# Expert slots spread over partitions, output weights stored by column halves, and TensorE kept active before the experts

## The chip, the cores and the metric

One Trainium2 chip, of which the kernel uses one core: TensorE (PE; its weight loads are PEld), VectorE (DVE), ScalarE (ACT), GpSimd (POOL), SyncE (SP, which here only issues DMAs) and 16 DMA engines. The metric is the device time of one execution in microseconds (us). What a measurement of this kernel can tell from no change is about 0.2%, some 3 us.

## The reference

One decoder layer over 1024 tokens (and 16 meta tokens), model width 1024: attention and a gated recurrence, merged by gates; an output projection; then a hierarchical mixture of experts, and a last norm. All is float32. What matters here is the end:

```
merged = gate_m * (o_mla @ w_br_mla[l]) + gate_h * (o_hg @ w_br_hgrn[l])
h = h + merged @ w_out[l]
u = rmsnorm(h, ffn_norm[l])
h = h + hier_moe(u, ...)      # top group of 8, then the top 2 of its 8 experts
...
# hier_moe: a token's two experts e (of 64), each with w1, w3: 1024x256 and w2: 256x1024
hdn = jax.nn.silu(xb @ w1[e]) * (xb @ w3[e])
y   = (hdn @ w2[e]) * gate    # scattered back and added to the token
```

Each expert has 3 MiB of weights (2 MiB of w1 and w3, "up", 1 MiB of w2, "down"), 192 MiB in all, and they are read once from HBM. The inputs are drawn from a fixed seed, so the routing is fixed: 2048 (token, expert) pairs, on average 32 to an expert, 18 to 46.

## The kernel before

**Up to the experts.** The first half of the time goes to projections, attention and recurrence. `merge_part` makes the merged branches. `output_part` then runs over 8 tiles of 128 tokens. For a tile t, TensorE multiplies with the output weights in four quarters (`quarter`; each product is three matmuls, L130 to L132, of high and low parts; the weights' parts lie in `g.woh` and `g.wol`); quarters 0 and 1 give columns 0 to 511, quarters 2 and 3 columns 512 to 1023, and each half raises `w_mm` by one, so `w_mm` is 2t+2 when tile t is done. DVE adds the result to the residual (`add`), ACT and DVE norm it, TensorE transposes it (`turn`), multiplies with the router's weights (`logits`, L1850), and DVE and ACT choose experts and gates (`choose`, `shares`, `shared`, `valued`). The product of tile t+1 hides the routing of tile t; for tile 7 nothing hides it.

**Lists.** For each chosen pair the rank of the token within its expert is counted (`ranks`, L1858, L1859; DVE reads it in `place`). `place` compares a table of numbers with the rank and so makes a matrix with a one where the slot is; `lists` (L1865, L1867) multiplies it with the token numbers and gates. The result is a list for every expert: its slot numbers stand along the partitions, 64 to an expert (`CAP`), an even expert on partitions 0 to 63 and an odd one on 64 to 127. The table is `io128`, which holds 0 to 63 twice, so the token of rank r stands on partition r (or 64 + r).

**Experts.** `experts_part` takes two experts (a pair) at a time. GpSimd gathers the rows of a pair from `u_moe` in HBM by an indirect DMA (L1612, L2046: 128 indices, one 4 KiB row to each partition; indices beyond the range move nothing), TensorE transposes them (L2192), multiplies with w1 and w3 (L2219, 32 rows of the trace to an expert) and w2 (L2203), and GpSimd scatters the pair's results to `y_moe` by an indirect DMA (L2057). The weights come through 7 buffers (`NBUF`): `g.load_up` (two DMAs of 1 MiB, L1352) and `g.load_down` (one, L1356), both issued by SP. The first 7 experts' loads are issued in `output_part`'s `sync`; expert e+7 is loaded when expert e's products are done (`up_mm`, `dn_mm`). Each load spreads over all 128 partitions and all 16 DMA engines. After the last expert the rows of `y_moe` and `h_mid` are read back, added, normed and stored.

**Memory that holds back loads.** Up buffers 4 to 6 and down buffers 4 and 5 lie where `g.woh` and `g.wol` are, down buffers 3 and 6 where the merged tiles' parts `f_mh` and `f_ml` are. In the kernel before, none of these is loaded until `w_mm` is 16:

```
sp.wait_ge(w_mm, 2 * TT)
g.load_down(sp, 3, 3)
store_u(TT - 1)
g.load_up(sp, 4, 4)
```

**GpSimd before the first gather** writes the slot records of each tile (`record`, L1600, two indirect DMAs), clears one row buffer after tile 7's norm (L1606), waits for the lists (`rows_ok`) and gathers; a third buffer is cleared at L2028.

Of the kernel before, what the change touches and what calls it, by code (L numbers as in the profile page):

```python
# [15 lines left out]
F32 = mybir.dt.float32  # L16
# [1345 lines left out]
def merge_part(nc, g, sem):  # L1362
# [14 lines left out]
    wo_src = g.w_out[0].rearrange("(j p) n -> p j n", p=P)  # L1377

# [42 lines left out]
    def scalar(act):  # L1421
        def high(n):
            if n >= 2:
                act.wait_ge(mm_ok, done(n - 2, 1))
                act.wait_ge(w_in[n % 2], 16 * ((n - 2) // 2) + 16)
            act.activation(wh[n % 2][:, :, :], w[n % 2][:, :, :], ACT.Copy).then_inc(wh_ok, 1)

        def high_out(n):
            act.wait_ge(wo_in[n % 2], 16 * (n // 2) + 16)
            act.activation(g.woh[:, 2 * n:2 * n + 2, :], wo[n % 2][:, :, :], ACT.Copy).then_inc(woh_ok, 1)  # L1430

        high(1)
        for n in range(2, DK):
            high(n)
            if n < 6:
                high_out(n - 2)
# [29 lines left out]
    def merge_low_out(dve, n):  # L1466

        dve.wait_ge(woh_ok, n + 1)
        dve.tensor_tensor(g.wol[:, 2 * n:2 * n + 2, :], wo[n % 2][:, :, :], g.woh[:, 2 * n:2 * n + 2, :].bitcast(F32),
                          ALU.subtract).then_inc(wol_ok, 1)  # L1470
# [5 lines left out]
def output_part(nc, g, sem):  # L1476

# [5 lines left out]
    with ExitStack() as here:  # L1483
# [15 lines left out]
        io8, io128, tok, upper = sb("f_io8", [P, 8]), sb("f_io128", [P, 2, EXPERTS]), sb("f_tok", [P, TT]), sb("f_upper", [P, P])  # L1499
        srcf = sb("f_srcf", [P, PAIRS])  # L1500
# [14 lines left out]
        g.rows_ok = rows_ok  # L1515
        g.rec_out, g.most_ok = rec_out, sem("f_most_ok")
# [4 lines left out]
        def sync(sp):  # L1521
# [27 lines left out]
            for t in range(TT - 1):  # L1549
                store_h(t)  # L1550
                store_u(t)
                if t + 2 < TT:
                    sp.wait_ge(h_tr, 2 * t + 2)
                    sp.wait_ge(h_out[t % 2], 16 * (t // 2 + 1))
                    load_x(t + 2)
                if t == 0:
                    g.load_down(sp, 1, 1)
                    g.load_down(sp, 2, 2)
                elif t == 1:
                    sp.wait_ge(ml_ok, 4)  # L1560
                    g.load_up(sp, 2, 2)
                elif t == 5:
                    sp.wait_ge(ml_ok, TT)
                    g.load_up(sp, 3, 3)
            sp.wait_ge(w_mm, 2 * TT)
            g.load_down(sp, 3, 3)
            store_u(TT - 1)
            g.load_up(sp, 4, 4)
            store_h(TT - 1)
            g.load_down(sp, 4, 4)  # L1570
            for b in range(5, NBUF):
                g.load_up(sp, b, b)
                g.load_down(sp, b, b)

        def gpsimd(pool):
# [3 lines left out]
                      allow_small_or_imprecise_dtypes=True).then_inc(cst, 1)  # L1579
            pool.iota(tok[:, :], pattern=[[P, TT]], base=-int(SKIP), channel_multiplier=1,  # L1580
# [24 lines left out]
            pool.wait_ge(u_ok, TT)  # L1605
            pool.memset(xr[1], 0.0).then_inc(z_ok, 1)  # L1606
            pool.wait_ge(z_ok, XB - 1)
# [9 lines left out]
        def scalar(act):  # L1617
# [38 lines left out]
            def valued(t):  # L1656
                one = V[t % 2]
                if t == 0:
                    act.wait_ge(cst, 5)
# [10 lines left out]
            for t in range(TT):  # L1670
                square(t, 0)
                if t == TT - 1:
                    turned(t, 0)
                square(t, 1)
                root(t)
                if t < TT - 1:
                    turned(t, 0)
                turned(t, 1)
                if t + 2 < TT:
                    split(t + 2)  # L1680
                table(t, ACT.Exp, 1)
                shares(t)
                valued(t)
                table(t, ACT.Sqrt, 2)

        def vector(dve):
# [64 lines left out]
            def place(t):  # L1751
# [8 lines left out]
                for k in range(2):  # L1760
                    dve.tensor_scalar(Pm[:, k, :], io128[:, :, :].rearrange("p a s -> p (a s)"), rank[:, k:k + 1], None,
# [22 lines left out]
            dve.wait_ge(cst, 5)  # L1784
            for j in range(DK):
                dve.tensor_scalar(wr[:, j, :], wr[:, j, :], gT[:, j:j + 1], None, ALU.mult).then_inc(wr_ok, 1)
            for t in range(TT):
# [4 lines left out]
                if t == TT - 1:  # L1792
                    first_sum(t)
                if t:
# [24 lines left out]
        def tensor(pe):  # L1819
            def quarter(t, n):  # L1820
# [7 lines left out]
                for j in range(4 * (n % 2), 4 * (n % 2) + 4):  # L1828
                    last = mm3(pe, bank(2 * b + q), mh[b][:, j, :], ml[b][:, j, :], g.woh[:, j, q * 512:(q + 1) * 512],
                               g.wol[:, j, q * 512:(q + 1) * 512], j == 0, j == DK - 1)  # L1830
# [11 lines left out]
            def logits(t, q):  # L1842
                pe.wait_ge(hT_ok, 2 * t + q + 1)
# [26 lines left out]
            pe.wait_ge(cst, 5)  # L1870
# [19 lines left out]
            lists(TT - 2)  # L1890
            ranks(TT - 1)
            lists(TT - 1)
            pe.wait_ge(cum_ok, TT)
            pe.matmul(RK, g.ones[:, :], Mcum[:, :], start=True, stop=True).then_inc(rk_mm, 1)

# [3 lines left out]
def experts_part(nc, g, sem):  # L1899
# [4 lines left out]
    with ExitStack() as here:  # L1904
# [7 lines left out]
        x_zero = sem("m_x_zero")  # L1912
# [114 lines left out]
        def gpsimd(pool):  # L2027
            pool.memset(x[XB - 1], 0.0).then_inc(x_zero, 1)  # L2028
            pool.wait_ge(x_zero, 1)
# [298 lines left out]
def program(nc, a, out):  # L2328
# [8 lines left out]
    with ExitStack() as keep:  # L2337
# [62 lines left out]
        with ExitStack() as early:  # L2400
            g.woh = early.enter_context(nc.sbuf_tensor("woh", [P, DK, D], F32R, side="right"))
            g.wol = early.enter_context(nc.sbuf_tensor("wol", [P, DK, D], F32R, side="right"))
        for b in (4, 5, 6):
            r13[b] = right(f"r13_{b}", [P, 2, DK, DE])
            if b < 6:
                r2[b] = right(f"r2_{b}", [P, 2, D])
# [36 lines left out]
```

## Time and profile before

| | us |
|---|---|
| median of 3 runs | 1522.33 (1521.8 to 1523.7) |
| the profiled execution | 1522.54 |
| its span in the profile | 1520.7 |
| TensorE busy | 1380.3 (91%) |
| DVE busy, ACT busy | 583.1, 559.7 |

The span is the time from the first to the last record; 1.8 us of the profiled execution lie around it. The DMA digits of the page say how busy the 16 DMA engines were on the mean, in slices of 38 us: low up to slice 25, then 9 up to the end. A busy TensorE row doesn't say that TensorE is the bound: its matmuls are pipelined. The stages of this kernel have different bounds, so each is read by itself: the output projection (about 842 to 957 us of the span), the routing of tile 7 and the lists (to 971), the experts (980 to 1481), the last norm (to the end).

### The profile page before, as it was taken

Reading aid. Unit: us, or ns where it says so; the run is one execution under the profiler, and the core shown is the slowest. Engines: PE = TensorE matmul, PEld = TensorE weight load, DVE = VectorE, ACT = ScalarE, POOL = GpSimd, SP = SyncE. Lnnn points to the kernel's source line nnn. Section 1 sums busy time; section 2 is a strip of 40 time slices with the busy share of each in tenths; the row PEclk is TensorE's granted clock in tenths of the full one; section 3 lists DMA queues with packets and bytes.
Section 4 is the critical chain, followed back from the end, with each engine's and each line's share of the span. In section 5 each row is a group of like instructions: output and inputs, shape, how many; then the busy total and the mean of one; then the engine's idle time right before and its main releaser. Section 6 shows DMA issues by size and latency. Waiting matters only on the chain. (4 is left out here: it accounts for less than half of the span.)

```text
span 1520.7 us, 20875 instructions
## 1 busy us (share of the span) xinstructions
PE 1380.3 (91%) x8375; PEld 977.9 (64%) x8375; DVE 583.1 (38%) x1301; ACT 559.7 (37%) x1064; POOL 107.2 (7%) x129
## 2 busy tenths in 40 slices
PE   5999999999999998999998999599987888787877
PEld 5888887787888885766666888455543444443433
DVE  6455565422531144567666555411101011110117
ACT  5534344223331265454542455333322222222223
POOL 0000000000000000000000012211111111111100
PEclk9999999999999998999999999699999899999998
DMA  6111111112224333112128644799999999999988
GB/s 182 42 29 42 28 43 28 32 42 70 97 87 122 98 73 104 61 45 70 43 70 299 259 157 167 292 406 417 415 416 417 416 416 415 412 413 415 411 329 340
DMA packets 130592, 312.52 MB, mean 206 GB/s; under 512 B 31280, under 2 KB 77360, under 8 KB 113344
## 3 DMA queue, kind: packets, MB, share of 16 engines
q1 hardware_dynamic: 118464, 285.96, 50.1%
q0 software_dynamic: 12032, 25.22, 4.3%
q8 instruction: 67, 1.10, 0.3%
q14 instruction: 29, 0.24, 0.1%
HBM read 283.81 MB, written 41.98 MB: 214 GB/s over the span
## 5 line engine op out<-in xcount | busy, mean ns | idle before, releaser
L2219 PE MATMUL ps<-r,m_xT 128*64 128x256 f32 x2048 | 260.0, 411 | 71.9 <-DMA r<-in_w 70.6
L130 PE MATMUL ps<-uTh,h_wh 128*128 128x512 f32 (+3 forms) x696 | 263.7, 379 | 4.4 <-DVE uTl L557 2.4
L2219 PEld LDWEIGHTS ps<-r,m_xT 128*64 128x64 f32 x2048 | 153.4, 147 | 161.4 <-DMA r<-in_w 79.2
L131 PE MATMUL ps<-uTl,h_wh 128*128 128x512 f32 (+3 forms) x696 | 255.9, 368 | 0.0
L132 PE MATMUL ps<-uTh,h_wl 128*128 128x512 f32 (+3 forms) x696 | 255.6, 367 | 0.0
L2139 DVE TENSOR_TENSOR m_prod<-m_sig,ps 128x128 f32<-128x128 f32 x64 | 18.4, 288 | 346.0 <-ACT m_sig L2110 316.4
L130 PEld LDWEIGHTS ps<-uTh,h_wh 128*128 128x128 f32 (+1 forms) x696 | 129.4, 186 | 28.7 <-DVE uTl L557 4.3
L132 PEld LDWEIGHTS ps<-uTh,h_wl 128*128 128x128 f32 (+1 forms) x696 | 129.3, 186 | 20.1
L131 PEld LDWEIGHTS ps<-uTl,h_wh 128*128 128x128 f32 (+1 forms) x696 | 129.6, 186 | 19.4 <-issue 0.2
L2203 PE MATMUL ps<-r,m_hT 128*64 128x512 f32 x512 | 122.4, 598 | 1.3 <-DVE m_hT L2143 0.9
L2100 ACT ACTIVATE m_y<-ps,gate 64x512 f32<-64x512 f32 x128 | 87.3, 682 | 80.1 <-PE ps L2203 78.4
L562 DVE TENSOR_TENSOR h_wl<-h_w,h_wh 128x1024 fp32r<-128x1024 f32 (+2 forms) x43 | 51.0, 1185 | 166.9 <-ACT h_wh L386 166.9
L2110 ACT ACTIVATE m_sig<-ps 128x128 f32<-128x128 f32 x64 | 17.7, 277 | 254.6 <-PE ps L2219 244.0
L1250 PE MATMUL ps<-KT,QT 96*128 96x512 f32 (+3 forms) x192 | 75.7, 507 | 2.5 <-PEq L106 2.5
L1088 ACT ACTIVATE t_p<-ps,t_negmax 112x128 f32<-112x128 f32 (+7 forms) x64 | 47.4, 741 | 63.4 <-DVE t_negmax L1157 63.3
L418 ACT ACTIVATE h_sg<-ps,h_bias 128x512 f32<-128x512 f32 x32 | 22.0, 688 | 131.2 <-PE ps L132 131.2
L618 DVE SCALAR_TENSOR_TENSOR h_S<-h_S,h_dec,ps 128x128 f32<-128x128 f32 x124 | 43.0, 347 | 56.0 <-PE ps L899 46.1
L2203 PEld LDWEIGHTS ps<-r,m_hT 128*64 128x64 f32 x512 | 34.1, 136 | 46.3 <-issue 38.2
L2057 POOL DMA_INDIRECT y_moe<-m_y,dst x31 | 30.9, 997 | 407.1 <-ACT m_y L2100 390.8
L2143 DVE COPY m_hT<-ps 128x128 f32<-128x128 f32 x64 | 18.7, 292 | 102.6 <-PE ps L2230 102.1
L449 ACT ACTIVATE h_kdn<-ps 128x128 f32<-128x128 f32 x32 | 8.9, 278 | 128.9 <-PE ps L878 128.9
L1261 PE MATMUL ps<-ident,t_p 128*128 128x128 f32 (+1 forms) x288 | 45.6, 285 | 7.8 <-DVE t_p L1165 7.4
(355 smaller groups left out, 2087.1 us busy)
## 6 DMA issues: line engine op xcount, KB each, us to landing
r<-in_w SPq DMA_DIRECT2D x190, 1024.0 KB
h_w<-in_w_in SPq DMA_DIRECT2D x37, 512.0 KB, 4.1
gates<-h_sg POOLq DMA_DIRECT2D x16, 512.0 KB, 2.9
r<-y_moe SPq DMA_DIRECT2D x8, 1024.0 KB, 18.6
br_gate<-gates SPq DMA_DIRECT2D x14, 512.0 KB, 4.7
e_wo<-in_w_out SPq DMA_DIRECT2D x4, 1024.0 KB, 10.2
f_x<-in_x SPq DMA_DIRECT2D x8, 512.0 KB, 5.1
h_mid<-f_x SPq DMA_DIRECT2D x8, 512.0 KB, 3.0
```

The lines of the kernel that those rows point to most:

```text
L130: pe.matmul(out, lh, rh, start=start, stop=False)
L131: pe.matmul(out, lh, rl, start=False, stop=False)
L132: return pe.matmul(out, ll, rh, start=False, stop=stop)
L562: dve.tensor_tensor(used(wl, J), used(w, J), used(wh, J).bitcast(F32), ALU.subtract).then_inc(wl_ok, 1)
L618: dve.scalar_tensor_tensor(out=S[:, (n + 1) % 8, :], in0=S[:, n % 8, :], scalar=dec[:, n:n + 1], in1=bank(KVB(ci), 0, P), op0=ALU.mult, op ...
L1088: act.activation(pr[b][0:rows(i), 0:P * (i + 1)], score(b, i, 0, P * (i + 1)), ACT.Exp, bias=negmax[0:rows(i), b:b + 1], accum_out=total[0 ...
L1250: ins = pe.matmul(score(b, i, c, w), g.QT[:, h, qcol(i):qcol(i) + rows(i)], g.KT[:, h, c:c + w], start=True, stop=True)
L1261: ins = pe.transpose(g.ps[:, (T_BANK + tbank(i, b, gi)) * 512 + x * P: (T_BANK + tbank(i, b, gi)) * 512 + x * P + rows(i)], pr[b][0:rows(i ...
L2057: pool.indirect_dma_start(out=g.y, out_offset=bass.IndirectOffsetOnAxis(ap=g.dst[:, n:n + 1], axis=0), in_=y[n % XB][:, :], in_offset=None ...
L2100: act.activation(y[i % XB][CAP * k:CAP * (k + 1), q * 512:(q + 1) * 512], bank(Y_BANK + e % 2, 0, 512, CAP * q, CAP * (q + 1)), ACT.Copy, ...
L2203: ins = pe.matmul(bank(Y_BANK + e % 2, 0, 512, CAP * f, CAP * (f + 1)), hT[:, j, :], g.r2[b][:, j, 512 * f:512 * (f + 1)], start=j == 0, s ...
L2219: ins = pe.matmul(bank(UP_BANK + e % 2, 0, DE, CAP * f, CAP * (f + 1)).rearrange("p (r f) -> p r f", r=2), xT[i % 2][:, j, CAP * k:CAP * ( ...
```

## The change

Three things are changed. **Slots:** the table that `place` compares ranks with is `slot_of` instead of `io128`. Seen as 2 halves (k) of 2 x 8 x 2 x 2 numbers (a, g, r, q), partition 64k + 32a + 4g + 2r + q gets the rank 32a + 7 - g + 16r (q = 0) or 32a + 8 + g + 16r (q = 1). So ranks 0 to 15 of an expert stand two to each group of four partitions in the first 32, ranks 16 to 31 fill these groups, and ranks 32 on do the same in the next 32. The slot records still use the rank. **Output weights:** `woh` and `wol` are stored as [q, j, 512], the halves q of their columns apart, and the buffers over them are laid out anew, so that up buffers 4 and 5 lie over half 0 (whose last use is at `w_mm` 15) and up 6, down 4 and down 5 over half 1. Down 3 is loaded from `w_mm` 14 on, up 4 and up 5 from 15 on, the rest from 16 on. **TensorE kept active:** `keep_up` issues matmuls of 128x128 whose result nobody reads: 16 before tile 7's ranks and 32 after the last lists. Beside these: for tile 7 DVE instead of ACT copies the second half of the transposed tile; ACT loads its square-root table before `valued` instead of behind it, in every tile; two row buffers are cleared by ACT after its last `valued`, and GpSimd's two memsets are gone.

```diff
-            act.activation(g.woh[:, 2 * n:2 * n + 2, :], wo[n % 2][:, :, :], ACT.Copy).then_inc(woh_ok, 1)
+            act.activation(g.woh[:, :, 2 * n:2 * n + 2, :], by_half(wo[n % 2]), ACT.Copy).then_inc(woh_ok, 1)
...
+        slot_of = sb("f_slot_of", [P, 2, 2, 8, 2, 2])
...
             for t in range(TT - 1):
+                if t == TT - 2:
+
+                    sp.wait_ge(w_mm, 2 * TT - 2)
+                    g.load_down(sp, 3, 3)
                 store_h(t)
                 store_u(t)
...
+            sp.wait_ge(w_mm, 2 * TT - 1)
+            g.load_up(sp, 4, 4)
+            g.load_up(sp, 5, 5)
             sp.wait_ge(w_mm, 2 * TT)
-            g.load_down(sp, 3, 3)
             store_u(TT - 1)
-            g.load_up(sp, 4, 4)
+            g.load_down(sp, 4, 4)
+            g.load_down(sp, 5, 5)
             store_h(TT - 1)
-            g.load_down(sp, 4, 4)
-            for b in range(5, NBUF):
-                g.load_up(sp, b, b)
-                g.load_down(sp, b, b)
+            g.load_up(sp, 6, 6)
+            g.load_down(sp, 6, 6)
...
+            for k in range(2):
+                pool.iota(slot_of[:, k, :, :, :, 0], pattern=[[32, 2], [-1, 8], [16, 2]], base=7, channel_multiplier=0,
+                          allow_small_or_imprecise_dtypes=True).then_inc(cst, 1)
+                pool.iota(slot_of[:, k, :, :, :, 1], pattern=[[32, 2], [1, 8], [16, 2]], base=8, channel_multiplier=0,
+                          allow_small_or_imprecise_dtypes=True).then_inc(cst, 1)
...
-            pool.wait_ge(u_ok, TT)
-            pool.memset(xr[1], 0.0).then_inc(z_ok, 1)
-            pool.wait_ge(z_ok, XB - 1)
+            pool.wait_ge(z_ok, XB)
...
+                table(t, ACT.Sqrt, 2)
                 valued(t)
-                table(t, ACT.Sqrt, 2)
+            act.wait_ge(u_ok, TT)
+            act.activation(xr[1], g.ones[:, 0:1].to_broadcast([P, D]), ACT.Copy, scale=0.0).then_inc(z_ok, 1)
+            act.wait_ge(lg_mm, TT)
+            act.activation(xr[2], g.ones[:, 0:1].to_broadcast([P, D]), ACT.Copy, scale=0.0).then_inc(z_ok, 1)
...
-                    dve.tensor_scalar(Pm[:, k, :], io128[:, :, :].rearrange("p a s -> p (a s)"), rank[:, k:k + 1], None,
+                    dve.tensor_scalar(Pm[:, k, :], slot_of[:, :, :, :, :, :].rearrange("p k a g r q -> p (k a g r q)"),
+                                      rank[:, k:k + 1], None,
                                       ALU.is_equal).then_inc(P_ok, 1)
...
                 if t == TT - 1:
                     first_sum(t)
+                    dve.wait_ge(h_tr, 2 * TT)
+                    dve.wait_ge(lg_mm, TT - 1)
+                    dve.tensor_copy(hT[:, 4:8, :], bank(5).rearrange("p (j t) -> p j t", j=4)).then_inc(hT_end, 1)
...
+            def keep_up(n):
+
+                for _ in range(n):
+                    pe.matmul(bank(1, 0, P), g.ident[:, :], g.ones[:, :], start=True, stop=True)
...
             lists(TT - 2)
+            keep_up(16)
             ranks(TT - 1)
             lists(TT - 1)
             pe.wait_ge(cum_ok, TT)
             pe.matmul(RK, g.ones[:, :], Mcum[:, :], start=True, stop=True).then_inc(rk_mm, 1)
+            keep_up(32)
...
-            pool.memset(x[XB - 1], 0.0).then_inc(x_zero, 1)
-            pool.wait_ge(x_zero, 1)
```

SP's queue, from the load of up buffer 3 to that of up buffer 6; r_3 to r_6 are the buffers, 128x2048 x2 an up load, 128x2x1024 a down load. Before:

```order
L1352 DMA r_3<-in_w 128x2048 x2
L1527 DMA h_mid<-f_x 128x1024
L1531 DMA u_moe<-f_u 128x1024
L1356 DMA r_3<-in_w 128x2x1024
L1531 DMA u_moe<-f_u 128x1024
L1352 DMA r_4<-in_w 128x2048 x2
L1527 DMA h_mid<-f_x 128x1024
L1356 DMA r_4<-in_w 128x2x1024
L1352 DMA r_5<-in_w 128x2048 x2
L1356 DMA r_5<-in_w 128x2x1024
L1352 DMA r_6<-in_w 128x2048 x2
L1356 DMA r_6<-in_w 128x2x1024
```

The same place now:

```order
L1352 DMA r_3<-in_w 128x2048 x2
L1356 DMA r_3<-in_w 128x2x1024
L1533 DMA h_mid<-f_x 128x1024
L1537 DMA u_moe<-f_u 128x1024
L1352 DMA r_4<-in_w 128x2048 x2
L1352 DMA r_5<-in_w 128x2048 x2
L1537 DMA u_moe<-f_u 128x1024
L1356 DMA r_4<-in_w 128x2x1024
L1356 DMA r_5<-in_w 128x2x1024
L1533 DMA h_mid<-f_x 128x1024
L1352 DMA r_6<-in_w 128x2048 x2
L1356 DMA r_6<-in_w 128x2x1024
```

Down 3 moved ahead of tile 6's stores, up 4 and up 5 ahead of tile 7's store to `u_moe` (the second L1531, now L1537).

TensorE, from tile 7's second transposition to the first expert, now (before, the two L1901 rows are not there, and the rest stands in the same order):

```order
L1864 MATMUL ps<-ident,f_x 128x128 x4
L1878 MATMUL ps<-f_wr,f_hT 128x72 x8
L1893 MATMUL ps<-f_V,f_Pm 128x192
L1895 MATMUL ps<-f_V,f_Pm 128x128
L1901 MATMUL ps<-ones,ident 128x128 x16
L1886 MATMUL ps<-f_Ms,f_upper 128x64
L1887 MATMUL ps<-f_Mcum,ones 128x64
L1893 MATMUL ps<-f_V,f_Pm 128x192
L1895 MATMUL ps<-f_V,f_Pm 128x128
L1928 MATMUL ps<-f_Mcum,ones 128x64
L1901 MATMUL ps<-ones,ident 128x128 x32
L2224 MATMUL ps<-ident,rows 128x128 x8
```

The 16 stand ahead of tile 7's ranks (L1886, L1887), the 32 ahead of the first transposition of gathered rows (L2224, before L2192), so both can hold back what is behind them.

## Rows read from the trace of the kernel before

**Rows 1.** The page's DMA digits and the chain that ended last, by engine.
```profile
DMA  6111111112224333112128644799999999999988
...
PE 19%; DMA 16%; SPq 8%; DVE 3%; issue 1%; ACT 1%; POOLq 0%; DVEq 0%; ACTq 0%
```

**Rows 2.** Stretches: busy time by engine, granted clock, DMA share, GB/s.
```profile
950.00:956.00 6.00, 6.00 (x31) 5.03 (x31) 4.21 (x22) 1.67 (x7) 0.00 (x0) 1.00 0.00 0
956.00:985.00 29.00, 11.47 (x62) 9.29 (x62) 11.37 (x51) 11.18 (x24) 9.55 (x9) 0.62 0.89 334
965.00:970.00 5.00, 2.45 (x9) 2.27 (x10) 3.10 (x20) 2.86 (x7) 0.00 (x0) 0.50 0.96 307
985.00:990.00 5.00, 4.99 (x35) 3.33 (x31) 0.57 (x2) 0.41 (x2) 1.93 (x2) 0.80 1.00 407
1000.00:1100.00 100.00, 100.00 (x726) 54.20 (x727) 14.17 (x49) 35.28 (x65) 16.16 (x16) 1.00 1.02 413
1465.00:1470.00 5.00, 3.47 (x31) 2.38 (x29) 0.87 (x3) 1.17 (x3) 0.99 (x1) 1.00 0.69 277
1470.00:1475.00 5.00, 3.66 (x24) 1.41 (x20) 0.00 (x0) 1.36 (x2) 0.00 (x0) 1.00 0.28 92
1490.00:1500.00 10.00, 10.00 (x25) 4.50 (x24) 9.37 (x12) 4.81 (x11) 0.00 (x0) 1.00 1.02 420
```

**Rows 3.** One stretch, L2219 alone: PE and PEld busy, clock, DMA, GB/s.
```profile
1136.50:1448.10 311.60, 155.60 (x1184) 90.77 (x1184) 0.93 1.02 414
```

**Rows 4.** TensorE in order of time, the last expert, then the adding.
```profile
1472.02 1.95 PE L2219 MATMUL ps<-r,m_xT 128*64 128x256 f32 x16 [0.31 <-DMA r<-in_w]
1475.42 1.95 PE L2219 MATMUL ps<-r,m_xT 128*64 128x256 f32 x16 [1.45 <-DMA r<-in_w]
...
1486.97 1.88 PE L2265 MATMUL ps<-r,ident 128*128 128x512 f32 x4
```

**Rows 5.** SP's queue in order of time.
```profile
956.67 0.38 SPq L1356 DMA_DIRECT2D r<-in_w  x1
961.19 0.32 SPq L1531 DMA_DIRECT2D u_moe<-f_u  x1
961.55 1.27 SPq L1352 DMA_DIRECT2D r<-in_w  x2
...
968.93 1.02 SPq L1356 DMA_DIRECT2D r<-in_w  x1
988.77 0.80 SPq L1352 DMA_DIRECT2D r<-in_w  x2
```

**Rows 6.** The chain of waits in order of time: start, us, what.
```profile
962.56 1.71 DVE f_not L1724
966.44 0.69 PE ps L1858 x2
968.66 1.01 PE ps L1865 x2
971.45 8.45 DMA rows<-u_moe,src
980.04 1.96 PE ps L2192 x8
982.02 1.09 ACT m_xT L2089 x2
983.25 5.50 PE ps L2219 x32
990.15 3.60 PE ps L2219 x32
```

**Rows 7.** All engines in order of time around the last routing.
```profile
956.68 0.69 DVE L1698 TENSOR_TENSOR f_x<-f_x,ps 128x512 f32<-128x512 f32 x1 [0.59 <-PE ps L132]
...
963.26 0.96 POOL L1606 MEMSET rows<- 128x1024 f32 x1
...
967.27 0.59 ACT L1665 ACTIVATE f_V<-f_V,rec 128x64 f32<-128x64 f32 x2 [0.26 <-DVE rec L1749]
```

More of the change, by code:

```diff
@@ L1377, in merge_part @@
     wo_src = g.w_out[0].rearrange("(j p) n -> p j n", p=P)
+    by_half = lambda one: one[:, :, :].rearrange("p j (q n) -> p q j n", q=2)
     other = [g.br_gate[n][:, 1, :] for n in range(2)]
@@ L1468, in merge_low_out @@
         dve.wait_ge(woh_ok, n + 1)
-        dve.tensor_tensor(g.wol[:, 2 * n:2 * n + 2, :], wo[n % 2][:, :, :], g.woh[:, 2 * n:2 * n + 2, :].bitcast(F32),
+        dve.tensor_tensor(g.wol[:, :, 2 * n:2 * n + 2, :], by_half(wo[n % 2]), g.woh[:, :, 2 * n:2 * n + 2, :].bitcast(F32),
                           ALU.subtract).then_inc(wol_ok, 1)
@@ L1515, in output_part @@
         g.rows_ok = rows_ok
+        hT_end = sem("f_hT_end")
         g.rec_out, g.most_ok = rec_out, sem("f_most_ok")
@@ L1658, in valued @@
                 if t == 0:
-                    act.wait_ge(cst, 5)
+                    act.wait_ge(cst, 9)
                 act.wait_ge(M_ok, t + 1)
@@ L1677, in scalar @@
                     turned(t, 0)
-                turned(t, 1)
+                    turned(t, 1)
                 if t + 2 < TT:
@@ L1783, in vector @@
             dve.wait_ge(cst_in, 96)
-            dve.wait_ge(cst, 5)
+            dve.wait_ge(cst, 9)
             for j in range(DK):
@@ L1828, in quarter @@
                 for j in range(4 * (n % 2), 4 * (n % 2) + 4):
-                    last = mm3(pe, bank(2 * b + q), mh[b][:, j, :], ml[b][:, j, :], g.woh[:, j, q * 512:(q + 1) * 512],
-                               g.wol[:, j, q * 512:(q + 1) * 512], j == 0, j == DK - 1)
+                    last = mm3(pe, bank(2 * b + q), mh[b][:, j, :], ml[b][:, j, :], g.woh[:, q, j, :], g.wol[:, q, j, :],
+                               j == 0, j == DK - 1)
                 if n % 2:
@@ L1842, in logits @@
             def logits(t, q):
-                pe.wait_ge(hT_ok, 2 * t + q + 1)
+                if (t, q) == (TT - 1, 1):
+                    pe.wait_ge(hT_end, 1)
+                else:
+                    pe.wait_ge(hT_ok, 2 * t + q + 1)
                 if q == 0:
@@ L1868, in lists @@
                           start=False, stop=t == TT - 1).then_inc(oh_mm, 1)
[L1870 removed]
+            def keep_up(n):
+                for _ in range(n):
+                    pe.matmul(bank(1, 0, P), g.ident[:, :], g.ones[:, :], start=True, stop=True)
+            pe.wait_ge(cst, 9)
             for n in range(4):
@@ L2400, in program @@
         with ExitStack() as early:
[L2401 to L2406, printed above, removed]
+            g.woh = early.enter_context(nc.sbuf_tensor("woh", [P, 2, DK, 512], F32R, side="right"))
+            g.wol = early.enter_context(nc.sbuf_tensor("wol", [P, 2, DK, 512], F32R, side="right"))
+        r13[6], r13[4] = right("r13_6", [P, 2, DK, DE]), right("r13_4", [P, 2, DK, DE])
+        r2[4], r2[5] = right("r2_4", [P, 2, D]), right("r2_5", [P, 2, D])
+        r13[5] = right("r13_5", [P, 2, DK, DE])
         g.r13, g.r2 = [r13[b] for b in range(NBUF)], [r2[b] for b in range(NBUF)]
```

1 line of the change is left out of this document (removed).

## The prediction

> **What bounds the kernel now.** I read the page first, then the chain of waits in order of time, then a table of stretches, then SP's queue. The page says where to look: the DMA engines are at 9 tenths from slice 26 on, and DMA with SP's queue makes 24% of the chain [rows 1]. The table says it sharply: from 1000 to 1100 us, and again from 1136.5 to 1448.1, the DMA share is 1.02 at 413 and 414 GB/s [rows 2, 3]. A share of 1.02 is as full as it gets here; in the last stage 1.02 goes with 420 GB/s [rows 2]. So the experts are bound by bytes: a TensorE that is ready waits for weights. Time can be won there in only two ways: start the flow of bytes earlier, or have it end earlier for the same bytes.
>
> Two views show such room. At the front the DMA share is 0.00 from 950 to 956 [rows 2], because the loads of the buffers over the output weights wait for tile 7 [rows 5]. At the end, TensorE still waits for the last expert's weights at 1472.02 and 1475.42 [rows 4], while the mean DMA share is 0.69 (1465 to 1470) and 0.28 (1470 to 1475) [rows 2]. Engines idle on the mean while a transfer is awaited that all 16 share: some DMA engines are late, others done.
>
> **How uneven the engines are.** Each weight load gives all 16 engines the same. The gathered and scattered rows need not: an expert with 32 tokens fills partitions 0 to 31 only, and an expert with 20 leaves 20 to 31 empty. The new table treats four neighbouring partitions, with the four 32 above, as one group, 16 groups in all. Suppose that a group is what one DMA engine serves. The routing of the reference's fixed inputs gives, over all 64 experts, 70 to 180 rows to a group before, 121 to 132 after; the mean is 128. Each row moves twice (gather, scatter), 8192 bytes.
>
> Is it so? One stretch tests it. Between 1136.5 and 1448.1 TensorE did 1184 rows of L2219 [rows 3], which at 32 each is 37 experts (23 to 59) in 311.6 us. An engine moves 420/16 = 26.25 GB/s [rows 2], so 8.18 MB in that time. Weights are 37 x 3 MiB / 16 = 7.27 MB; 0.91 MB is left, 110 rows. The busiest group has 114 in these experts, the mean 76. At the mean the stretch would have taken 300.8 us. With rows dealt by partition number modulo 16 the busiest has 94 (306.4 us), with eight neighbours to an engine 152 (324.5 us). Groups of four give 312.7 against 311.6 seen. Taking the stretch's own 414 GB/s instead, 96 rows are left, so modulo 16 isn't shut out.
>
> The Trainium skill states this grouping outright ("SBUF — State Buffer", Door 1: The DMA port swizzle; "DMA: Bandwidth & Descriptors", The descriptor swizzle): partitions p and p+32 of a block of four share a port, and one engine serves it. By that rule the busiest engine is the one worked out above, and the trace agrees as far as the 110 rows go; no row names a single engine.
>
> **Part 1, slots.** DVE compares with another table of the same 128 numbers: no cost. The four iotas run long before. The busiest engine goes from 180 rows to 132: 48 x 8192 B / 26.25 GB/s = **15.0 us** less until the last weights are there. The stage after it, reading `y_moe` and `h_mid` back, is even over the engines and starts for the late engine when it is done, so it shifts as a whole. Bounds: 10 us from the end alone (shares short of 1.02 from 1465 to 1475 are 0.33 x 5 + 0.74 x 5 = 5.4 us of mean idling, plus 1.5 MiB of the next stage, 3.8 us, which early engines can do meanwhile, and about 1 us in the mid-stage); 16 us if the late engine drops to the very mean (52 rows). I take 14.5, since the rows of the first pair and the last scatter don't all lie in the bound part.
>
> **Part 2, loads earlier.** Ten loads of 1 MiB are issued from 956.67 to 968.93 [rows 5]. With the stores of tile 7 (1.05 MB) and two gathers (0.47 MB) that is 12.0 MB. From 956 to 985 the DMAs moved 29 x 334 = 9.7 MB [rows 2]; the other 2.3 MB at 410 GB/s last until 990.6. At 988.77 SP already issues expert 7's load [rows 5], so the flow never breaks, and the weights from expert 7 on begin at 990.6.
> Now: down 3 goes a tile earlier, up 4 and up 5 when half 0 of tile 7 is multiplied. Before the end of tile 7, which SP sees at 956.67 [rows 5], lie two quarters, 24 matmuls at 6.00/31 us each [rows 2], and some 2 us of small products: about 950. These 5 MiB are 12.6 us of transfer, 4 MiB of them from 950 on, done by 960. The other five, with the stores, are 6.3 MB and start at 961 or so: done by 977. But then all 7 buffers are full, and the flow waits for expert 0's products. The 12.6 us are not won; what is won is how much earlier than 990.6 expert 7's load can start.
>
> **Part 3, the way to the first expert.** This sets that moment. Step by step, before against now:
> - DVE's copy for tile 7 comes ahead of `place` and the norm. Nearest row: 0.69 us for 128x512 from PSUM [rows 7]. It takes the place of ACT's copy, which came later; net 0.5 later.
> - `f_not` took 1.71 us for 128x8 numbers [rows 6] and ended at 964.27, when GpSimd's memset (963.26 + 0.96) did [rows 7]. The memset is gone, a slot record remains in the way: 0.4 to 1.0 less, with the 0.5 above taken off.
> - Ranks, lists and the counts run at clock 0.50 [rows 2]; L1858 0.69 and L1865 1.01 [rows 6] halve with the 16 matmuls ahead of them. Price of one: 512 columns take 1.88/2 = 0.94 [rows 4], 128 columns 0.235; 16 are 3.8 us, in the wait that ends at 966.44. Some 1.0 less in all.
> - But the gather also waits for the cleared buffers, now two ACT passes over 1024 elements, 1.09 each [rows 6], behind the last `f_V` (967.27 + 0.59 [rows 7], give or take 0.5). Cleared at 970, where the lists were ready at 970.5. So only 0.3 to 1.0 of the gain is kept: gather at 970.8 for 971.45.
> - The gather took 8.45 to land [rows 6] among weights at full share; now the backlog ends near 977. I take 8.0; bounds 6.5 and 8.5.
> - The 32 matmuls: 32 x 0.235 = 7.5 us from 970, done at 977.5, before the rows land at 978.8. The clock stays: transposition 1.09 for 1.96, products 3.60 for 5.50 [rows 6].
> Expert 0 is done at 978.8 + 0.1 + 1.1 + 1.2 + 0.1 + 3.6 = 984.9; first bytes a microsecond later, 985.9. **Gain 4.7, say 5 us.** Bounds: 9 (gather 6.5, zeroing hidden) and 1 (32 matmuls at half clock, 15 us, until 985, which hold up the transposition).
>
> ACT's reordering puts a table load (1.3 us) into a wait; TensorE bounds those tiles, so nothing. The new layout of `woh` changes no size. GpSimd's later memset goes: the zero scatter is 2 us earlier, awaited by nobody.
>
> **Sum.** 14.5 + 5 = 19.5 us off the profiled 1522.54; the median of the runs is 1522.33, so **1503 us**.
>
> **Rivals.**
> 1. *Only the front* (1517). The bound is the memory's rate, elastic over engines, and light engines' time is used anyhow. For: the share is 1.02, never visibly short before 1450. Against: the waits of 1472 and 1475 with a share of 0.28. 1522.3 - 5. The skill's "DMA: Bandwidth & Descriptors", Where 436 GB/s comes from, has HBM bind a core's loads at about 358 GB/s, which would make this rival right; the measured 414 to 420 disagrees.
> 2. *Only the balance* (1508). The front's gain is lost: the 32 matmuls at half clock, or the gather no earlier. 1522.3 - 14.5.
> 3. *Slower* (1526). Rows are dealt by partition number modulo 16. Then the new table, which puts ranks 0 to 15 on partitions 0 and 1 of each four, raises the busiest from 156 to 173 rows: 17 x 8192 / 26.25 = 5.3 us more, and with the front at its lower bound of 1 the kernel is 4.3 us slower. It decides once the front gives under 2.3 us. For: one of the two readings above, 96 rows, is near its 94. Against: the other, 110.
> 4. *More* (1496): 16 and 9, with a little from the cleared mid-stage.
>
> **Chances.** Forecast (1499 to 1506) 0.64; rival 4 0.13; rival 2 (1506 to 1511) 0.12; rival 1 0.06; rival 3's mechanism 0.05, of which half comes out within 0.2% (the front pays for it) and 0.02 slower. A measurement can tell 0.2%, 3 us, from no change. Faster 0.94, same 0.03, slower 0.03. Range: 1495 to 1511, which leaves out rival 1, rival 3 and a little of rival 4.
>
> **What the profile after would show.** Slots: 37 experts from 23 to 59 in 301 to 303 us, and a DMA share that stays near 1 until TensorE's last wait for weights, where 0.28 stood. If the stretch still takes 311, the first term is wrong; if 317, rival 3. Loads: a share well over 0 from 950 to 956, a dip between 977 and 985, and expert 7's load issued near 985. Clock: 1.00 from 965 on, first products 3.6 us. If the first L2219 starts after 984, the way to the first expert was mis-sized. The forecast fails as a whole if TensorE bounds the experts after all; it takes 990.15 - 983.25 = 6.9 us for one with the clock just risen [rows 6], against 3.41 MB / 420 GB/s = 8.1 for the bytes.

## The result, and the profile after

The changed kernel takes **1511.42 us** (median; 1511.23 to 1511.78) where the kernel before takes 1522.91 on the same chip: ratio 0.9924, 95% interval 0.9911 to 0.9936. That is 11.5 us gained, where 19.5 were forecast (1503 us); the time lies just above the range. The profiled execution took 1511.23 us, its span is 1509.5 us.

Where the gain arises is read from the start of an expert's first product, in the trace in order of time:

| expert | before | after | lead, us |
|---|---|---|---|
| 0 | 983.25 | 981.63 | 1.6 |
| 18 | 1094.86 | 1093.10 | 1.8 |
| 23 | 1136.59 | 1131.80 | 4.8 |
| 60 | 1448.18 | 1437.33 | 10.9 |
| 63 | 1472.02 | 1461.73 | 10.3 |
| span | 1520.7 | 1509.5 | 11.2 |

Up to expert 18 TensorE doesn't wait for weights (both kernels have it 100.00 busy from 1000 to 1100), so only its own earlier start shows, not a lead in the flow of bytes. By expert 23 the weights set the pace, and 4.8 us are there; the next 37 experts add 6.1, the rest 0.3.

The page of the kernel after, which answers to [rows 1]:

```profile
DMA  6111111112224333121109664989999999999998
...
PE 20%; DMA 16%; SPq 7%; DVE 3%; issue 1%; ACT 1%; POOLq 0%; DVEq 0%
```

A slice is now 37.7 us, not 38.0, so that the stretches aren't quite the same; what counts is the 9 for 7 in slice 26 (943 to 981), the earlier loads, and the 9 for 8 in the last slice but one: the end is fuller.

Its stretches (us, busy PE, PEld, DVE, ACT, POOL, granted clock, DMA share, GB/s), which answer to [rows 2]:

```profile
950.00:956.00 6.00, 6.00 (x38) 5.24 (x37) 3.20 (x18) 1.88 (x4) 0.00 (x0) 1.00 0.95 255
965.00:970.00 5.00, 3.17 (x18) 2.85 (x17) 3.64 (x23) 4.30 (x8) 0.00 (x0) 0.82 0.88 235
980.00:990.00 10.00, 8.72 (x61) 6.11 (x61) 0.86 (x3) 3.73 (x6) 2.05 (x2) 0.83 0.58 207
1000.00:1100.00 100.00, 100.00 (x727) 53.97 (x725) 13.85 (x48) 35.17 (x65) 16.15 (x16) 1.00 1.02 412
1460.00:1465.00 5.00, 3.44 (x28) 1.59 (x26) 0.00 (x0) 1.36 (x2) 0.00 (x0) 1.00 0.95 361
1465.00:1470.00 5.00, 3.45 (x21) 1.25 (x17) 0.87 (x3) 0.28 (x1) 0.00 (x0) 1.00 1.02 422
```

Two things came as forecast: the flow runs from 950 to 956, and while TensorE waits for its last weights (1460 to 1465) the share is 0.95, where 0.28 stood. Two did not, or not quite: the clock from 965 to 970 is 0.82 for 1.00, and the dip of the flow, forecast between 977 and 985, lies between 980 and 990 (207 GB/s).

The stretch of experts 23 to 59, L2251 (was L2219) alone, which answers to [rows 3]:

```profile
1131.70:1437.20 305.50, 158.45 (x1184) 92.13 (x1184) 0.92 1.02 416
```

305.5 us for 311.6; 301 to 303 were forecast. TensorE is still the one that waits in it (us in total, times, longest); before and after:

```profile
PE ps L2219 <- DMA r<-in_w: 60.1, 33, 3.2
PE ps L2251 <- DMA r<-in_w: 51.2, 28, 3.3
```

The last expert on TensorE (answers to [rows 4]), in order of time:

```profile
1461.73 1.95 PE L2251 MATMUL ps<-r,m_xT 128*64 128x256 f32 x16 [0.98 <-DMA r<-in_w]
...
1464.26 1.95 PE L2251 MATMUL ps<-r,m_xT 128*64 128x256 f32 x16 [0.58 <-DMA r<-in_w]
```

SP's queue (answers to [rows 5]): down 3 at 942.96, up 4 and 5 at 949.87, up 6 with down 6 up to 965.95, and expert 7's load, the end of the dip.

```profile
942.96 0.38 SPq L1356 DMA_DIRECT2D r<-in_w  x1
...
949.87 1.85 SPq L1352 DMA_DIRECT2D r<-in_w  x4
...
965.95 0.68 SPq L1356 DMA_DIRECT2D r<-in_w  x1
987.02 0.80 SPq L1352 DMA_DIRECT2D r<-in_w  x2
```

The chain of waits (start, us, what), answering to [rows 6]:

```profile
967.77 0.60 PE ps L1893 x2
968.38 0.44 PE ps L1895 x2
...
970.24 8.85 DMA rows<-u_moe,src
...
979.23 1.15 PE ps L2224 x8
980.40 1.09 ACT m_xT L2121 x2
981.63 5.36 PE ps L2251 x32
```

All engines in order of time, answering to [rows 7]:

```profile
963.58 0.23 DVE L1745 TENSOR_SCALAR f_not<-f_io,f_sc 128x8 f32<-128x8 f32 x1
...
968.27 1.04 ACT L1705 ACTIVATE rows<-ones 128x1024 f32<-128x1024 f32 x1
968.92 8.67 PE L1901 MATMUL ps<-ones,ident 128*128 128x128 f32 x64
```

The gather is issued at 970.24 (forecast 970.8), but takes 8.85 us to land. The 32 matmuls that nobody reads (two records of the trace to each) end at 977.6, TensorE idles 1.6 us, and the first expert's products take 5.36 us for a forecast 3.6, the clock being at its lower level for part of them. Of the 1.2 us by which the gather is issued earlier than in [rows 6], 0.4 is lost in the landing.

### The profile page after: what moved, and what is told of

It is laid out like the page before. It is cut to its first block and busy times, and to the rows that moved or that the text cites. A ratio compares the mean times of both kernels' runs of the same rounds, so it can differ in the third digit from the quotient of the medians.

```text
span 1509.5 us, 21072 instructions
## 1 busy us (share of the span) xinstructions
PE 1392.3 (92%) x8471; PEld 989.9 (66%) x8471; DVE 581.9 (39%) x1302; ACT 560.8 (37%) x1065; POOL 102.2 (7%) x131
## 5 line engine op out<-in xcount | busy, mean ns | idle before, releaser
L2251 PE MATMUL ps<-r,m_xT 128*64 128x256 f32 x2048 | 259.6, 411 | 62.8 <-DMA r<-in_w 61.6
L2251 PEld LDWEIGHTS ps<-r,m_xT 128*64 128x64 f32 x2048 | 153.1, 147 | 151.9 <-DMA r<-in_w 70.2
```

The lines of the kernel that those rows point to most:

```text
L2251: ins = pe.matmul(bank(UP_BANK + e % 2, 0, DE, CAP * f, CAP * (f + 1)).rearrange("p (r f) -> p r f", r=2), xT[i % 2][:, j, CAP * k:CAP * ( ...
```

## The experiments

"Rows" below is, as in the prediction, the number of gathered rows in the busiest group of four partitions, in all 64 experts or in the stretch of 37. Times are medians; a gain in us is (1 - ratio) x 1523. The length of the stretch is read from one profiled execution. With the slots of the changed kernel, seven profiled executions (after, e2, e6, e7, e8, e11, e12) have it at 303.8 to 305.9 us, so a difference under some 2 us between two stretches says nothing.

**e1, e2, e3: the two parts by themselves, and the table mirrored.** In e1 the changed kernel has the old order of slots (180 rows, 114 in the stretch); e3 puts rank r on 31 - r, so other engines are the full ones. e2 is the kernel before with `slot_of` alone.

```diff
 # e1
-                pool.iota(slot_of[:, k, :, :, :, 0], pattern=[[32, 2], [-1, 8], [16, 2]], base=7, ...
-                pool.iota(slot_of[:, k, :, :, :, 1], pattern=[[32, 2], [1, 8], [16, 2]], base=8, ...
+                pool.iota(slot_of[:, k, :, :, :, :].rearrange("p a g r q -> p a (g r q)"), pattern=[[32, 2], [1, 32]], base=0, ...
 # e3
+                pool.iota(... the same ..., pattern=[[32, 2], [-1, 32]], base=31, ...
 # e2, against the kernel before
-                    dve.tensor_scalar(Pm[:, k, :], io128[:, :, :].rearrange(...), rank[:, k:k + 1], None,
+                    dve.tensor_scalar(Pm[:, k, :], slot_of[:, :, :, :, :, :].rearrange(...), rank[:, k:k + 1], None,
```

> The changed kernel with the old slot order (rank r on partition r), all else as changed. Theory A (a DMA engine serves a group of four partitions, and the busiest engine sets the time, 26.25 GB/s): 180 rows for 132, 15 us slower than the changed kernel, 1526. Theory B (A holds, but one of the engines that had few rows is slower by itself, so that evening out won only half): about 7 to 8 us slower, 1519. Theory C (the slots win nothing, all came from the front): 1511.

Measured: 1520.26 us, ratio 0.9981 (0.9971 to 0.9990). The stretch:

```profile
1135.00:1446.10 311.10, 155.87 (x1184) 91.15 (x1184) 0.93 1.02 414
```

With the old slots the stretch is the old one. The parts for the front are worth 2.9 us by themselves, not 5.

> The kernel before with the new slot table alone. Theory A: 1522.5 - 15 = 1508. Theory B: 1522.5 - 7 to 8 = 1515. Theory C: 1522.5. With e1 it shows whether the slots and the rest add up.

Measured: 1515.8 us, 0.9955 (0.9941 to 0.9969). The stretch:

```profile
1135.10:1439.42 304.32, 148.99 (x1184) 87.75 (x1185) 0.96 1.02 416
```

The slots alone give 6.9 us, not 14.5. The two parts sum to 9.8, the change gives 11.5: each is worth 1.7 more beside the other, about what the intervals leave open.

> The changed kernel with the old order mirrored: rank r on partition 31 - r of its 32, so the groups that had 70 and 86 rows now have 165 and 180, and the busiest is as busy as in e1 (180). Theory A (all engines alike): the same as e1 within 1 us. Theory B (the last group's engine, which had few rows, is the slow one): slower than e1, by the 7 us that B gives to that engine. If the slow engine were the first one: faster than e1.

Measured: 1521.81 us, 0.9986 (0.9976 to 0.9995). As e1 within the intervals, stretch 311.3. So it doesn't matter which engines are full, and no single slow engine explains the old time: e2's 1515.8 is what theory B named, but e3 refutes its reason.

**e4: the rows concentrated.** Eight consecutive ranks to a group of four partitions: six groups with 246 to 256 rows, 152 in the stretch.

```diff
+                pool.iota(... p a g (r q) ..., pattern=[[4, 2], [8, 8], [1, 4]], base=0, ...
```

> The changed kernel with ranks 0 to 7 on the first group of four partitions (and the four 32 above), 8 to 15 on the second, and so on: the busiest group has 256 rows, the last two none. Theory A: 76 rows more than e1 at 0.312 us, 24 us slower than e1, 39 us slower than the changed kernel: 1550. If rows were dealt by partition number modulo 16 or the rate were shared elastically, much less than that: under 10 us over e1.

Measured: 1549.89 us, 1.0173 (1.0156 to 1.0189), 29.6 us over e1. The stretch:

```profile
1147.20:1474.40 327.20, 162.70 (x1184) 93.81 (x1184) 0.91 0.99 387
```

This speaks against rival 3. Dealt by partition number modulo 16, e4's busiest engine would have 173 rows, as many as the changed kernel's, and both would be some 5 us slower than e1, which has 156. But the changed kernel is 8.8 us faster than e1 and e4 29.6 slower, as groups of four say. One reading of size fails too: e4 costs 0.39 us for each row over 180, while e1 against the changed kernel is 8.8 us for 48 rows, 0.18 each. At 26.25 GB/s a row is 0.31. The price of a row is not one number.

**e5 and e13: in between.** e5 has 147 rows (90 in the stretch), e13 has 158 (98; its eight fuller engines have 138 to 158).

```diff
 # e5
+                pool.iota(slot_of[:, k, :, 0:7, :, :]..., pattern=[[32, 2], [1, 7], [7, 4]], base=0, ...
+                pool.iota(slot_of[:, k, :, 7, :, :]..., pattern=[[32, 2], [1, 4]], base=28, ...
 # e13
+                for f in range(2):
+                    pool.iota(slot_of[:, k, :, 4 * f:4 * f + 4, :, :]..., pattern=[[32, 2], [1, 4], [4, 4]], base=16 * f, ...
```

> The changed kernel with a table that is uneven in between: seven groups of a half share the ranks, the eighth gets ranks 28 to 31 and 60 to 63, so the busiest has 147 rows, two have 70 and 86. Theory A (the busiest engine alone sets the time): 15 rows more than the changed kernel, 4.7 us at 0.312, 5.8 us at the 0.39 a row that e1 and e4 give: 1516 to 1517. Theory D (two bounds: the busiest engine at 0.39 us a row, and all engines together at the 416 GB/s of the stage, which binds once the rows are even): under some 157 rows the second one binds, so 1511.4, as the changed kernel. Theory B (the engines of the last groups are slow by themselves): faster than the changed kernel, since these have fewer rows.

Measured: 1514.63 us, 0.9944 (0.9927 to 0.9961). The stretch:

```profile
1132.10:1438.30 306.20, 155.83 (x1184) 90.99 (x1184) 0.93 1.02 415
```

> The changed kernel with a table of two levels: in each half, four groups share ranks 0 to 15 (and 32 to 47), four the ranks 16 to 31 (48 to 63): busiest 158 rows, 145 to 158 on eight engines, 101 to 116 on the other eight. The line of e9, e10, e4 and the changed kernel (280.0 us of weights and 0.33 us a row from expert 23 to 60, some 93 rows) gives 310.7 us for the stretch and 8 us more than the changed kernel, 1520. If uneven tables beat that line unless many engines stand idle, as the old order does by 5 us: 306 to 308, 1515 to 1517.

Measured: 1516.77 us, 0.9948 (0.9931 to 0.9964). The stretch:

```profile
1134.50:1442.80 308.30, 153.58 (x1185) 89.93 (x1185) 0.94 1.02 416
```

From 82 rows on the stretch takes 305.5, 306.2, 308.3 and (e1) 311.1. The first step is within what equal tables differ by, the second at its edge; the rise as a whole is clear of it. A slope of 0.31 us a row, taken down from 311.5 at 114 rows, would have had 304.0 for e5 and 306.5 for e13. Theory D of e5 (1511.4) lies just outside its interval, theory B (faster than the changed kernel) well outside.

**e9, e10, e14: fewer rows.** e9 moves none, e10 only the first group's of each half (2 engines of 16, with 114 and 96 in the stretch; 14 have nothing), e14 only four groups' of each half (8 engines with 72 to 114 rows, 8 without). In all three `y_moe` is filled early from `x` by two DMAs, since the scatters no longer fill it. Their first expert starts 7 to 8 us later than in the changed kernel (988.51, 990.04 and 988.86), so only the stretch is compared.

```diff
 # e9
+                pool.iota(... p a (g r q) ..., pattern=[[0, 2], [0, 32]], base=-1, ...
 # e10
+                pool.iota(slot_of[:, k, :, 0, :, :]..., pattern=[[32, 2], [1, 4]], base=0, ...
+                pool.iota(slot_of[:, k, :, 1:8, :, :]..., pattern=[[0, 2], [0, 28]], base=-1, ...
 # e14
+                pool.iota(slot_of[:, k, :, 0:4, :, :]..., pattern=[[32, 2], [1, 16]], base=0, ...
+                pool.iota(slot_of[:, k, :, 4:8, :, :]..., pattern=[[0, 2], [0, 16]], base=-1, ...
```

> The changed kernel with a table that matches no rank: the lists are empty, so no row of tokens is gathered or scattered, and the experts' contribution is left out; y_moe is filled early with two copies of x (8 MiB, before attention), which lengthens no later stage. Read by the stretch of TensorE's up products from expert 23 to expert 60 (311.6 us before, 305.5 after). 116.4 MB of weights alone. All engines bound together at 416 GB/s: 279.8 us. The port rate of 27.2 GB/s an engine that a fit of a constant cost a row gives (0.39 us a row): 267.4. At 420 GB/s, the rate that the prediction used: 277.

Measured: one run, 1483.59 us. The stretch:

```profile
1131.30:1411.30 280.00, 147.74 (x1184) 87.19 (x1184) 0.96 1.02 413
```

Weights alone: 7.27 MB to an engine in 280.0 us is 26.0 GB/s, 416 in all (the 413 of the row counts what moved in just these us). 16 engines with equal work don't reach 16 x 26.25 = 420 here.

> As e9, but ranks 0 to 3 and 32 to 35 stand on the first four partitions and on 32 to 35 (the old order for this group alone); all other rows of tokens are left out. Two engines carry 180 and 165 rows, as in e1 and before, the other 14 weights alone. If an engine has a rate of its own, whatever the others do: the stretch is as long as in e1, 311 us. If the engines share a bound: shorter, as the others leave it room; at 27.2 GB/s on the busy engine (7.27 + 0.93 MB) 302. If rows were not dealt by groups of four: near e9.

Measured: one run, 1534.86 us. The stretch:

```profile
1142.80:1460.60 317.80, 158.37 (x1184) 92.03 (x1184) 0.92 0.98 373
```

14 engines have 11% fewer bytes than the fullest one (7.27 for 8.21 MB), the total falls to 373 GB/s, and the stretch is not shorter but 6 us longer. The trace's landing records of one weight load agree: each of 16 engines marks its part, 14 of them within some 2 us, two 11 to 18 us later (expert 22's down load: 14 from 1114.4 to 1116.1, two at 1127.3 and 1128.8). Dealt modulo 16, these rows would have made four engines late. Note the share: 0.98. It doesn't tell engines that have less to move; the GB/s do.

> As e10, but the first four groups of each half keep their rows in the old order (ranks 0 to 15 and 32 to 47), so eight engines carry 128 to 180 rows and eight the weights alone; rows of the other ranks are left out. The stretch was 311.1 with all rows (e1) and 317.8 with one group (e10), with the same 180 on the busiest. If the busiest engine is slowed the more, the more engines wait for it: between the two, 313 to 316. If only the loads of its own engine count: as e1 or as e10.

Measured: one run, 1528.55 us. The stretch:

```profile
1142.70:1454.20 311.50, 157.06 (x1184) 91.61 (x1184) 0.93 1.01 395
```

With 8 engines lightened the full ones are as fast as in the kernel before (311.6), at 395 for 414 GB/s. So light neighbours don't by themselves slow the full ones; what made e10 slower is not found. The landing records name the groups once more: 8 engines mark expert 22's down load from 1113.5 to 1115.0, the other 8 from 1125.2 to 1128.8. Modulo 16 gives all 16 engines rows here, and with eight neighbours to an engine four would be full. Two late engines in e10 and eight in e14 fit groups of four alone, so this, with e4, settles rival 3.

**e6, e7, e8: the front, by parts.** e6 has SP's loads in the old order, e7 leaves out `keep_up`, e8 holds the last three loads until the first gather has landed.

```diff
 # e6
-            sp.wait_ge(w_mm, 2 * TT - 1)
-            g.load_up(sp, 4, 4)
-            g.load_up(sp, 5, 5)
 ... (as in the kernel before)
 # e7
-            keep_up(16)
-            keep_up(32)
 # e8
+            sp.wait_ge(g.x_in[0], 16)
             g.load_up(sp, 6, 6)
             g.load_down(sp, 6, 6)
```

> The changed kernel with SP's loads in the old order (none over the output weights before w_mm 16), all else as changed. By bytes the flow reaches expert 7 at 990.6, as before, for 987.5: 3 us slower, 1514.5. If the earlier loads win nothing (expert 7's load is set by expert 0's end alone): 1511.4.

Measured: 1515.71 us, 0.9949 (0.9933 to 0.9966): undoing the order costs 3.8 us by the ratios, though the intervals touch (against e11, the changed kernel again, they don't, and it is 5.2). In its chain the gather takes 8.13 us, and the clock stays up, although TensorE idles 1.02 us behind its 32 matmuls:

```profile
969.02 8.13 DMA rows<-u_moe,src
977.29 1.15 PE ps L2219 x8
979.69 3.67 PE ps L2246 x32
```

So e6 is done with expert 0 at 983.36, 3.6 us before the changed kernel, issues expert 7's load as much earlier (983.39 for 987.02), and is slower all the same: expert 23 starts at 1135.8 for 1131.8. Its queue still holds the late loads (406 GB/s from 980 to 990), so an earlier issue moves no byte earlier.

> The changed kernel without the 16 and the 32 matmuls. The first products were at half clock in the changed kernel anyway (5.36 us). If the matmuls are worth their ranks and lists (0.9 us) and the transposition (0.8 us): 1.7 us slower, 1513.1. If they are worth nothing, because the cleared buffers are awaited: 1512.2. If they cost (hold up something): faster than 1511.

Measured: 1514.15 us, 0.9939 (0.9923 to 0.9956); 2.3 us by the ratios, but the interval covers the changed kernel's. The trace has the reason for a small cost. Its chain:

```profile
966.15 0.69 PE ps L1886 x2
...
971.15 8.21 DMA rows<-u_moe,src
979.50 1.96 PE ps L2222 x8
...
982.71 6.22 PE ps L2249 x32
```

The clock is 0.50 from 965 to 985. Expert 0's products end at 988.9 for 987.0: 1.9 us.

> The changed kernel with the loads of up 6 and down 6 held until the first gather has landed. The DMA engines stood idle from 980 to 987 in the changed kernel, while the gather (8.85 us to land) shared them with these loads. If the gather is slow by sharing: it lands in 5 to 6 us, expert 0 ends 3 us earlier, the held 3 MiB (7.6 us) fill the hole: 3 us faster, 1508.5. If the gather's time is its own: it lands as late, the 3 MiB run from 979 to 987, and the time is the same, 1511.4.

Measured: 1507.82 us, 0.9896 (0.9879 to 0.9912): a version better than both. SP's queue:

```profile
975.98 0.84 SPq L1352 DMA_DIRECT2D r<-in_w  x2
...
982.98 0.81 SPq L1352 DMA_DIRECT2D r<-in_w  x2
```

GpSimd's gather, and the chain behind it:

```profile
969.79 1.04 POOL L1628 DMA_INDIRECT rows<-u_moe,src  x1 [5.69 <-DVE dst L1839]
```

```profile
968.39 8.74 PE ps L1902 x64
977.13 0.89 PE ps L2225 x8
...
979.28 3.67 PE ps L2252 x32
```

The gather lands at 976.0, 6.2 us behind its issue for 8.85. The transposition stands ready behind the 32 matmuls, with no gap, and the products take 3.67 us. Expert 0's are done at 982.95 for 986.99, and expert 7's load goes at 982.98 for 987.02. The flow from 980 to 990, in e8:

```profile
980.00:990.00 10.00, 9.99 (x80) 6.19 (x78) 1.47 (x6) 2.29 (x6) 1.32 (x2) 1.00 1.02 415
```

415 GB/s where the changed kernel has 207: the 3 MiB that were held come in the time that was empty anyway, and the gather no longer shares the engines with them.

**e11, e12: the changed kernel and e8 again**, in five rounds side by side, without further edits.

> The changed kernel again, for its time beside e12 on one chip: 0.992 of before.

Measured: 1511.61 us, 0.9915 (0.9901 to 0.9928).

> The kernel of e8 (up 6 and down 6 held until the first gather has landed) again, in more rounds: 0.990 of before and 3 to 4 us faster than the changed kernel beside it. If e8 was a lucky one: the same as e11.

Measured: 1508.1 us, 0.9892 (0.9877 to 0.9907). That is 3.5 us less than e11 on the same chip, and the slowest of e12's four executions (1509.17) is faster than the fastest of e11's five (1510.35); e8 and the first run of the changed kernel are 3.6 apart. The gather lands 7.0 us behind its issue in e12 (971.20 to 978.23), 8.75 in e11.

## Why the prediction was wrong

**The step that failed: "48 x 8192 B / 26.25 GB/s = 15.0 us less", by "An engine moves 420/16 = 26.25 GB/s".** The rate was taken from the last stage [rows 2] and held against one case, the uneven stretch before. The forecast used it for the even case as well, where it asks for 420 GB/s in all. No run has this stretch above 416. The rows of the kernel before already bounded the term: the 37 experts need 126.35 MB (weights and 1215 rows), and at the stretch's own 414 GB/s [rows 3] that is 305.2 us, at 416 it is 303.7. 305.5 was measured, and 303.8 to 305.9 in all runs with these slots. "At the mean the stretch would have taken 300.8" was no floor.

Why is there so little to win, when the engines are so uneven? Before, 311.6 us x 414 GB/s are 129.0 MB, 2.7 MB more than these experts need. The engines with few rows didn't idle: they ran ahead with later experts' weights, up to what 7 buffers allow. By the landing records of a down load, the first engine is 3 us ahead of the last at the start and some 18 from expert 42 on. After, it is 305.5 x 416 = 127.1 MB. So 1.9 MB or 4.6 us of the gain is less running ahead, and the rest of the 6.1 us is the rate, 416 for 414.

By place, with the rows of the group that is furthest behind at each point (180 at the end before, 132 after), all from profiled executions:

| | rows less | forecast at 0.312, us | e1 to after | before to e2 |
|---|---|---|---|---|
| up to the start of expert 23 | 11 | 3.4 | 3.3 | 1.5 |
| the stretch, 23 to 59 | 30 | 9.4 | 5.5 | 7.3 |
| from expert 60 on | 7 | 2.2 | 0.2 | -0.1 |
| in all | 48 | 15.0 | 9.0 | 8.7 |

So the term was mis-sized: 14.5 forecast; 6.9 alone (e2), 8.7 beside the rest (after against e1), by the medians' ratios. The front, forecast at 5, was near. The stretches by experiment:

| | rows, busiest | stretch, us | its rate, GB/s | in all, GB/s |
|---|---|---|---|---|
| no rows (e9) | 0 | 280.0 | 25.98 | 413 |
| after | 82 | 305.5 | 26.01 | 416 |
| e5 | 90 | 306.2 | 26.17 | 415 |
| e13 | 98 | 308.3 | 26.20 | 416 |
| before | 114 | 311.6 | 26.34 | 414 |
| e14 | 114 | 311.5 | 26.35 | 395 |
| e10 | 114 | 317.8 | 25.83 | 373 |
| e4 | 152 | 327.2 | 26.04 | 387 |

"Its rate" is (7.27 MB + rows x 8192 B) / the stretch. It differs by 2% over the table, which sounds little; but 1% of 311 us is 3 us, and the slots were to bring 9 or 10 there.

**What stays open.** Part of the 2% is the count. In the old order the busiest group of the stretch is not the one that is furthest behind when it starts: over experts 0 to 22 it has 50 rows, and another group, with 96 in the stretch, has 61. e10's trace shows the two change places: its two late landings of a down load are 1.8 us apart at expert 15, 0.4 at expert 29 and 3.6 at expert 50. So from start to start the last engine adds 103 rows, not 114, and moved 26.05 GB/s, not 26.34; the check in the prediction, 312.7 for 311.6, fitted by luck, as too high a rate and too many rows cancelled. Counted so, e3, e14, e9, e5 and e13 have 25.96 to 26.08 too, and one rate of 26.0 GB/s to an engine gives their stretches and the one before within 1 us. It is 2.7 us too low for after (73 rows, 25.77), 2.0 for e4 (144, 25.84) and 5.6 for e10 (25.55). No run tells why, nor why e14 and e10, with the same two full engines, are 6 us apart. Nor does one tell whether each engine has a limit of 26.0 or all together one of 416, since 16 x 26.0 is 416: in e4, e10 and e14, where the total falls to 373 to 395, the full engines are no faster than 26.1. One thing that evening out can't remove is seen in e9: without any row the spread of the landings still grows from 1 to 6 us, for 1 to 8 in the changed kernel.

**Point by point.**
- *A group of four partitions, with the four 32 above, is one DMA engine*: shown, by e4 (1.0173) and by the late landings of e10 and e14, and e3 shows that the engines are alike. The Trainium skill ("DMA: Bandwidth & Descriptors", The descriptor swizzle) states this grouping, and the runs agree.
- *The end*: the sign came, the gain did not. The last weights are awaited at a share of 0.95 for 0.28, but the lead goes from 10.9 us at expert 60 to 10.3 at expert 63: the fuller end shortens nothing.
- *Rival 1* (memory binds, elastic; 1517) is wrong by e2's 6.9 us. But its reason, that light engines' time is used anyhow, is half the answer: it was, up to the end of the buffers. The same page of the Trainium skill, section Where 436 GB/s comes from, puts the ports' ceiling at about 436, which is an estimate of 27.2 to an engine. The 416 and 26.0 here lie below it, and above the 358 at which the page has HBM bind.
- *Rival 3* (1526) is refuted by e4, e10 and e14. *Rival 4* is out. *Rival 2* (1508), in which the front gives nothing, names a time that is nearer to the measured one, for another reason: the front gives 2.9 to 4.7 us and the slots fall short.
- *Loads earlier*: the flow from 950 on came, and e6 puts it at 3.8 us. The reasoning that it is the load of expert 7 that counts holds where the queue ahead of it is empty: 987.02 for 988.77 [rows 5], and 982.98 in e8. In e6, with the queue full, an issue at 983.39 won nothing.
- *The way to the first expert*: forecast done at 984.9, measured 986.99. `f_not` is 0.23 us for 1.71, as forecast, and 1.71 again in e2, which keeps the memset: it ends at 964.73, the memset at 964.70. The Trainium skill ("SBUF — State Buffer", SBUF: two separate sides) has VectorE and GpSimd share a port pair that one instruction holds whole; the two common ends agree with it (before, 964.27 and 964.22), though `f_not` starts 0.7 us ahead of the memset, which no run explains. GpSimd's slot record, which runs beside `f_not` in the changed kernel (from 963.58), doesn't hold it up. The gather was 0.6 us earlier than thought. What was mis-sized: 8.0 for the landing, measured 8.85. It rested on a backlog that ends near 977, but the share is 1.02 up to 980; every run with these loads ahead of or beside the gather has 8.1 to 9.4, e8 and e12 without them 6.2 and 7.0. And "the clock stays", which rested on rows landing at 978.8 behind matmuls that end at 977.5. They landed at 979.1, TensorE idled 1.65 us, and the clock fell to 0.69 (980 to 985). It fell in e11 too (1.55 us idle), and stayed at 1.00 in e6 (1.02 us) and e8 (no gap).
- *Clock 1.00 from 965 on*: wrong, 0.82 from 965 to 970. The small products gained less than half, as the clock rose among them: L1893, before L1865, took 0.60 for 1.01 [rows 6]. With the clock at 0.50 (e7) it is 1.01 again.
- The front as a whole: 5 forecast, 2.9 (e1) to 4.7 (after against e2) measured, inside its bounds of 1 and 9.

The range was too narrow for the same reason: 10 us was taken as the least that the slots could give, from idle shares at the end which were read as time to be won whole. The direction of each part was right; it is the size of the slots' term that failed.

## What to carry to other kernels

Before pricing an uneven load by its busiest engine, divide the bytes that the stage needs by the total rate that the stage itself shows. That is about the time that evening out leaves. Here it says 305.2 us, and runs with even slots have 303.8 to 305.9, where the busiest engine's bytes promised 9 or 10 us and 6 came. Engines with less to do may have used their time to run ahead; a full share and buffers that allow it are the sign. Count rows from the start of the queue, not only in the stretch, and by groups of four partitions with the four 32 above, whenever indirect DMAs fill partitions unevenly. And where a small transfer sets a start, try letting the bulk loads behind which it lies wait for it, if there is an empty stretch later in which they fit: it gave 3.5 us here.

## What was not expected of the hardware

- The DMA share doesn't show engines with less to move: 0.98 in e10, where 14 of 16 engines have 11% less to move and the total is 373 GB/s.
- The price of a row on the busiest engine differs: 0.18 us between 132 and 180 rows, 0.39 between 180 and 256 (e4).
- The first gather took 8.85 us to land with the last 3 MiB of loads issued ahead of it, 6.2 and 7.0 (e8, e12) with these held back; 3.5 us of the whole time hang on it.
- By the landing records of a down load, the spread from the first engine to the last grows from 3 to 18 us over the experts in the kernel before, where it then stays, and from 1 to 8 after: the unevenness of all experts adds up until the buffers end it. Without any row (e9) it still grows from 1 to 6.
